# Last layer of a two-layer decoder step: the residual stream and the branch are transposed separately and leave in eight stores

## The reference, cut to what matters

```python
def rms_norm(x, g):
    y = xf * lax.rsqrt(jnp.mean(xf * xf, axis=-1, keepdims=True) + EPS)
    return (y * g).astype(x.dtype)

def cross_sublayer(x, mem_k, mem_v, lp):
    ...
    y = jnp.einsum("bshe,hed->bsd", o, lp["w_xo"])      # 512 -> 2048
    return x + rms_norm(y, lp["norm_x_post"])
```

## Time and profile before

| | us |
|---|---|
| median of the runs | 1278.66 |
| profiled execution, its own time | 1275.5 |
| its span, first to last instruction | 1273.8 |
| PE busy in the span | 1186.9 (93%) |
| DVE busy | 888.9 (70%) |
| ACT busy | 637.2 (50%) |
| POOL busy | 164.7 (13%) |

### The profile page before, as it was taken

The page is one execution under the profiler, slowest core; times in us unless marked ns, Lnnn a source line. Parts: engine busy times, 40 slices in busy tenths (PEclk is TensorE's granted clock), DMA queues, the critical chain, the costliest instruction groups (busy, mean ns, idle before and its releaser), DMA issues. The chain is left out here.

```text
span 1273.8 us, 25083 instructions
## 1 busy us (share of the span) xinstructions
PE 1186.9 (93%) x9846; PEld 1089.3 (86%) x9846; DVE 888.9 (70%) x1527; ACT 637.2 (50%) x1099; POOL 164.7 (13%) x278
## 2 busy tenths in 40 slices
PE   5999999999989899998799999999998999999893
PEld 5999999999767899986689999999976789999782
DVE  4679888888757444765677988888886644457635
ACT  5483444444547344554656544444445644446551
POOL 2200101010352000121011010101034300003100
PEclk8998999999999899999989999999999989999997
DMA  8964646474575466795356674646465646669611
GB/s 223 250 164 119 182 130 186 129 190 116 148 217 169 143 180 177 205 291 188 100 131 184 175 213 132 174 133 176 131 190 159 202 119 170 190 173 298 227 35 68
DMA packets 317544, 216.08 MB, mean 170 GB/s; under 512 B 21476, under 2 KB 300368, under 8 KB 316618
## 3 DMA queue, kind: packets, MB, share of 16 engines
q1 hardware_dynamic: 300624, 166.74, 47.4%
q0 software_dynamic: 16480, 47.73, 12.0%
q10 hardware_dynamic: 330, 0.11, 0.0%
HBM read 209.31 MB, written 7.15 MB: 170 GB/s over the span
## 5 line engine op out<-in xcount | busy, mean ns | idle before, releaser
L1810 DVE TENSOR_TENSOR wlo<-stage,whi 128x2048 fp32r<-128x2048 f32 x140 | 320.4, 2289 | 175.2 <-ACT whi L1227 175.1
L1227 ACT ACTIVATE whi<-stage 128x2048 fp32r<-128x2048 f32 (+2 forms) x159 | 274.6, 1729 | 312.9 <-PE U L651 252.7
L649 PE MATMUL U<-Ahi,whi 128*128 128x264 f32 x1152 | 334.4, 290 | 9.8 <-issue 8.0
L650 PE MATMUL U<-Alo,whi 128*128 128x264 f32 x1152 | 328.5, 285 | 0.0
L651 PE MATMUL U<-Ahi,wlo 128*128 128x264 f32 x1152 | 328.0, 285 | 0.0
L649 PEld LDWEIGHTS U<-Ahi,whi 128*128 128x128 f32 x1152 | 219.3, 190 | 10.9 <-issue 8.2
L650 PEld LDWEIGHTS U<-Alo,whi 128*128 128x128 f32 x1152 | 219.5, 191 | 0.0
L651 PEld LDWEIGHTS U<-Ahi,wlo 128*128 128x128 f32 x1152 | 218.1, 189 | 0.0
L1969 DVE SCALAR_TENSOR_TENSOR acc<-uext,cwall,acc 128x256 f32<-128x256 f32 x464 | 188.5, 476 | 0.1
L649 PE MATMUL U<-Bhi,whi 128*128 128x264 f32 x384 | 108.9, 284 | 0.0
L650 PE MATMUL U<-Blo,whi 128*128 128x264 f32 x384 | 108.8, 283 | 0.0
(11 more groups left out here) (415 smaller groups left out, 2206.0 us busy)
## 6 DMA issues: line engine op xcount, KB each, us to landing
stage<-in_w_in SPq DMA_DIRECT2D x76, 1024.0 KB, 5.9
stage<-in_w_out SPq DMA_DIRECT2D x32, 1024.0 KB, 6.2
stage<-in_w_mk SPq DMA_DIRECT2D x8, 1024.0 KB, 6.4
cp<-in_cache_kv_latent POOLq DMA_DIRECT2D x64, 128.0 KB, 3.0
cp<-in_cache_kv_latent SPq DMA_DIRECT2D x64, 128.0 KB, 2.9
stage<-in_w_mv SPq DMA_DIRECT2D x8, 1024.0 KB, 5.6
Kt<-in_cache_mem_k POOLq DMA_DIRECT2D x16, 512.0 KB, 4.9
stage<-in_w_xq SPq DMA_DIRECT2D x8, 1024.0 KB, 7.3
```

The costliest lines, as they stand in the source:

```text
L649: mm(bk[:, 0:cols], whi[:, s, w], hi[:, k, :], start=(k == 0), stop=False)
L650: mm(bk[:, 0:cols], whi[:, s, w], lo[:, k, :], start=False, stop=False)
L1227: return A_(out, in_, ACT.Copy, scale=scale)
L1810: ins = V.tensor_tensor(wlo[:, s, :], stage[:, s, :], whi[:, s, :].bitcast(F32), ALU.subtract)
```

## The change

In the last layer the transposition no longer waits for the finished sum. The stream `xT` (without this branch) is turned to token rows in eight pieces of 128 tokens x 512 features, one piece behind each of the blocks 1 to 8 of the output projection (`x_turn`), and DVE copies each piece into the row tiles `yR[0]`, `yR[1]`. After the last block the gained branch `yg`, not yet multiplied by the factor, is turned in the same eight pieces (`y_turn`), and DVE forms factor x branch + stream straight from the bank (`y_rows`), with the factor as one number per partition, since a token is now a partition. For that the sums of squares are made per token on partitions (columns 0 and 1 of `ST`) and, for the 8 sample tokens, as before (columns 2 to 9); root and reciprocal are 128 x 10 instead of 128 x 264. The sample tokens keep the old way in one multiply and one add over 16 x 8 elements, 16 transposes and four ACT copies. Every piece has its own store of 256 KB (rows of 2 KB), `ysN` a ninth store. Layer 0 is unchanged.

```diff
-    yN = at("yN", [P, 2, D], A0)
+    yR = [at(f"yR{t}", [P, D], (M, A0 + 4096)[t]) for t in range(2)]
...
+    def turn_bank(i):
+        return (HA, HB, HC, HD, HE)[i % 5]
...
-        sp.wait_ge(fin_act, 8)
-        sp.wait_ge(fin_dve, 8)
-        sp.dma_start(O["yp"].rearrange("a (t p) d -> p (a t) d", p=P), yN[:, :, :]).then_inc(st_y, 16)
+        y_d = O["yp"].rearrange("a (t p) d -> p (a t) d", p=P)
+        for i in range(8):
+            q, t = i // 2, i % 2
+            sp.wait_ge(fin_dve, 9 + i + (2 if i >= 2 else 0))
+            sp.dma_start(y_d[:, t, 512 * q:512 * q + 512], yR[t][:, 512 * q:512 * q + 512]).then_inc(st_y, 16)
+        sp.wait_ge(fin_act, 4)
         sp.dma_start(O["ys"].rearrange("b s d -> (b s) d"), ysN[:, :]).then_inc(st_y, 16)
-        sp.wait_ge(st_y, 32)
+        sp.wait_ge(st_y, 16 * 9)
...
+            def x_turn(i):
+                q, t = i // 2, i % 2
+                if i >= 5:
+                    pe.wait_ge(fin_dve, i - 4)
+                for c in range(4):
+                    last = tr(turn_bank(i)[:, c * P:(c + 1) * P], xT[:, 4 * q + c, t * P:(t + 1) * P], ident[:, :])
+                last.then_inc(fin_mm, 1)
...
                     last.then_inc(unit_done.sem if q == 3 else xo_mm.sem, 1)
-            squares(1)
-        pe.wait_ge(x_upd.sem, x_upd.at(L - 1, 8))
+                    if l == L - 1 and 1 <= bl <= 8:
+                        x_turn(bl - 1)
+            if l < L - 1:
+                squares(1)
+        def y_turn(i):
+            q, t = i // 2, i % 2
+            pe.wait_ge(u_evac.sem, u_evac.at(L - 1, U_XO + 4 * q + 4))
+            if i < 5:
+                pe.wait_ge(fin_dve, (6, 7, 8, 4, 5)[i])
+            elif i == 7:
+                pe.wait_ge(fin_dve, 9)
+            bk = (HA, HB, HC, HD, HE, U[0], U[1], HA)[i]
+            for c in range(4):
+                last = tr(bk[:, c * P:(c + 1) * P], yg[:, 4 * q + c, t * P:(t + 1) * P], ident[:, :])
+            last.then_inc(fin_mm, 1)
+        y_turn(0)
+        y_turn(1)
+        pe.wait_ge(std.sem, std.at(L - 1, 6))
+        pe.wait_ge(ssq_add.sem, ssq_add.at(L - 1, 28))
+        pe.wait_ge(sq_last.sem, sq_last.at(L - 1, 2))
+        for t in range(2):
+            mm(ST[:, t:t + 1], ssq[:, t * P:(t + 1) * P], ones[:, 0:1], start=True, stop=False)
+            mm(ST[:, t:t + 1], sqt[:, 3, t * P:(t + 1) * P], ones[:, 0:1], start=False, stop=True)
+        mm(ST[:, 2:2 + NB], ones[:, :], ssq[:, TP:T], start=True, stop=False)
+        mm(ST[:, 2:2 + NB], ones[:, :], sqt[:, 3, TP:T], start=False, stop=True).then_inc(stat.sem, 1)
+        for i in range(2, 8):
+            y_turn(i)
         pe.wait_ge(std.sem, std.at(L - 1, 7))
-        for c in range(KC):
...
+        pe.wait_ge(fin_dve, 12)
+        for q in range(4):
+            if q:
+                pe.wait_ge(fin_dve, (10, 13, 14)[q - 1])
+            for c in range(4):
+                last = tr((ST, HB, HC, HD)[q][0:NB, c * P:(c + 1) * P], xT[:, 4 * q + c, TP:T], ident[:, :])
+            last.then_inc(fin_mm, 1)
...
+        A_(stdS[:, 0:2 + NB], ST[:, 0:2 + NB], ACT.Sqrt, scale=1.0 / D, bias=epsv[:, 0:1]).then_inc(std.sem, 1)
+        for q in range(4):
+            act.wait_ge(fin_mm, 17 + q)
+            copy(ysN[:, 512 * q:512 * q + 512], (ST, HB, HC, HD)[q][0:NB, :]).then_inc(fin_act, 1)
...
             for bl in range(1, 15):
                 add_squares(1, bl)
+                if l == L - 1 and bl <= 8:
+                    i = bl - 1
+                    q, t = i // 2, i % 2
+                    dve.wait_ge(fin_mm, i + 1)
+                    V.tensor_copy(yR[t][:, 512 * q:512 * q + 512], turn_bank(i)[:, :]).then_inc(fin_dve, 1)
...
+        V.reciprocal(rs[:, 0:2 + NB], stdS[:, 0:2 + NB]).then_inc(rsq.sem, 1)
+        def y_rows(i):
+            q, t = i // 2, i % 2
+            row = yR[t][:, 512 * q:512 * q + 512]
+            dve.wait_ge(fin_mm, 9 + i)
+            V.scalar_tensor_tensor(row, (HA, HB, HC, HD, HE, U[0], U[1], HA)[i][:, :], rs[:, t:t + 1], row, ALU.mult, ALU.add
+                                   ).then_inc(fin_dve, 1)
+        y_rows(0)
+        y_rows(1)
+        dve.wait_ge(u_evac.sem, u_evac.at(L - 1, NG))
+        V.tensor_tensor(yg[:, :, TP:T], yg[:, :, TP:T], bc(rs[:, 2:2 + NB].unsqueeze(1), [P, KC, NB]), ALU.mult
+                        ).then_inc(fin_dve, 1)
+        dve.wait_ge(fin_dve, 11)
+        V.tensor_tensor(xT[:, :, TP:T], xT[:, :, TP:T], yg[:, :, TP:T], ALU.add).then_inc(fin_dve, 1)
+        for i in range(2, 8):
+            y_rows(i)
```

More of the change, by code:

```diff
@@ L1207, in _ @@
                     last.then_inc(unit_done.sem if q == 3 else xo_mm.sem, 1)
-            squares(1)
-        pe.wait_ge(x_upd.sem, x_upd.at(L - 1, 8))
-        pe.wait_ge(std.sem, std.at(L - 1, 7))
-        for c in range(KC):
[L1214 to L1219, removed]
+                    if l == L - 1 and 1 <= bl <= 8:
[25 more added lines that the diff above has]
+            y_turn(i)
+        pe.wait_ge(std.sem, std.at(L - 1, 7))
+        pe.wait_ge(fin_dve, 12)
[5 more added lines that the diff above has]
+            last.then_inc(fin_mm, 1)
     @block.scalar
@@ L1768, in _ @@
                 act.wait_ge(st_mk[e], l * 64 + 64)
[L1769 to L1775, removed]
+            if l < L - 1:
+                root(stat.at(l, 8), l, rsq.at(l, 6), 1.0 / D)
+        act.wait_ge(stat.sem, stat.at(L - 1, 8))
+        act.wait_ge(rsq.sem, rsq.at(L - 1, 6))
+        A_(stdS[:, 0:2 + NB], ST[:, 0:2 + NB], ACT.Sqrt, scale=1.0 / D, bias=epsv[:, 0:1]).then_inc(std.sem, 1)
+        for q in range(4):
+            act.wait_ge(fin_mm, 17 + q)
+            copy(ysN[:, 512 * q:512 * q + 512], (ST, HB, HC, HD)[q][0:NB, :]).then_inc(fin_act, 1)
     @block.vector
@@ L2403, in _ @@
                     lo(0, 0, ll=l + 1)
+            if l == L - 1:
+                break
             dve.wait_ge(u_evac.sem, u_evac.at(l, NG))
@@ L2407, in _ @@
                 residual(1, q)
-                if l + 1 < L and q:
+                if q:
                     next_lower(q - 1)
             assert ch.k == CHAIN_LAYER, ("CHAIN_LAYER", ch.k)
[L2412 to L2416, removed]
+        dve.wait_ge(std.sem, std.at(L - 1, 7))
+        V.reciprocal(rs[:, 0:2 + NB], stdS[:, 0:2 + NB]).then_inc(rsq.sem, 1)
+        dve.wait_ge(rsq.sem, rsq.at(L - 1, 7))
+        def y_rows(i):
[13 more added lines that the diff above has]
+            y_rows(i)
     block.__exit__(None, None, None)
```

## The result

The changed kernel took 1266.31 us in the median of five runs (1262.34 to 1267.96), beside 1278.58 us for five runs of the kernel before: the ratio is 0.9908 (95% interval 0.9889 to 0.9927). On the median that the prediction started from, this is 1266.9 us. Forecast were 1263.5 us and a range up to 1266.8. It is faster, as said, but by 3.4 us less, and the time lies a little outside the range. The profiled execution took 1266.42 us, with a span of 1264.7.

A forecast was written before the change was run, and what follows sets the result against it. Bounds: PE in the projection, then 30.65 us of PE, DVE and DMA in sequence. New end 1255.3 plus 3.3 for turns is 1258.6 against 1273.8; 15.2 off 1278.66 gives 1263.5 us, range 1260.8 to 1266.8.

The forecast's parts named there:

- The chain behind the projection: From the last product through factor, rows on DVE and stores: the span would end about 12.2 us after that product.
- The small products: Six PE products summing squares per token before the root: 0.11 us each, bounds 0.06 and 0.2.
- The rate of the stores: Moving each 256 KB piece out: 0.77 us, fast bound 0.66, slow bound 1.0.
- the gap: Between DVE's second and third pieces, two operations for the sample tokens: together 0.6 us.
- The landing: After the last byte: some 1.2 us until SP sees it landed, then the span's end, 1255.3.
- DVE's pieces: Eight row pieces formed on DVE after the factor: 0.74 us each, 0.66 when nothing is waited for.
- the sample tokens off the path: Their 16 transposes and ACT copies would end at about 1249.8, ahead of piece 7, hidden by DVE's work.
- The projection: Output projection, bound by PE: eight stream turns of 0.44 us, less 0.2 at block 8, lengthen it by 3.3 us.
- block 12's split: DVE's weight split for block 12 in the output projection: not late, by 0.6 us.
- The saving: Whole kernel: span end 1258.6 against 1273.8, 15.2 us less.
- the last step of the sum: Whole kernel: the 15.2 us saving taken off the earlier runs' median, 1278.66, giving 1263.5.
- the first rival: Turns at 0.66 us (+2.0), store pieces at 1.0 (+1.7), or both (+3.7): 1265.2 to 1267.2 us; chance 20%.

The follow-up runs named there:

- again_after: The changed kernel run once more, unaltered: 1262.70 us in the median of six runs, ratio 0.9885 to the kernel before.
- third_after: The changed kernel run again, unaltered, on the chip of later runs: 1264.13 us in the median of five runs, ratio 0.9887 to the kernel before.

## Why the prediction was right, and where it was wrong

**The chain behind the projection: right in sum, by errors that cancel.** The factor came 0.57 us late and the bytes took 0.54 longer, and the end behind the last byte took 0.8 less; of these, 0.3 are left. That the sum is so close is in part luck. All against the end of the last product:

| step | forecast, us | measured, us |
|---|---|---|
| factor ready | 2.25 | 2.82 |
| first store issued | 3.05 | 3.62 |
| first byte | 3.9 | 4.48 |
| last piece formed | 8.15 | 8.72 |
| last byte | 10.55 | 11.67 |
| end of the span | 12.15 | 12.46 |

- The small products were mis-sized. I took a transpose's 0.11 for each; they stand 0.22 us apart, since each is two matmuls (x2 in the rows above): 1.26 us for six, to the end of the last, where 0.83 was taken. That is a little over the upper bound of 0.2 for one. The turns ahead of them began 0.15 later than forecast.
- The rate of the stores was mis-sized a little: 7.19 us and not 6.65, which is 0.84 per piece for 0.77 once the gap and the small store are taken off. By the rate for 256 KiB in the Trainium skill, "SBUF — State Buffer", section "The DMA setup-cost knee", an estimate is 9.4: that rate is for one transfer at a time, and here several are under way, one issued every 0.66 us.
- The landing was mis-sized the other way: 0.8 us from the last byte to the end of the span, where 1.6 had been taken. This was a misreading of the kernel before: by its transfers' own records the burst ended 0.25 us before SP saw it landed, not 1.2, and 0.71 before the end of the span.
- DVE's pieces, their pitch of 0.66 and the sample tokens off the path came as forecast; the gap is 0.5 for 0.6.

**The projection: right.** 3.25 us more, 3.3 forecast; a turn costs 0.43 to 0.44, and nothing waits for block 12's split: DVE ends it at 1245.76, 0.55 before PE comes to the block.

**The saving: right in size, a little too large.** From the first product to the end the kernel before takes 54.39 and 53.25 us in its two profiles, the changed one 39.43, 39.45 and 39.44: 13.8 to 15.0 less, 15.2 forecast. The medians of the 40 runs of the kernel before that stood beside the experiments, 1278.34, and of all 16 of the changed one, 1263.57, differ by 14.8. That is as much as the stretch from the first product gives, so nothing is left for a delay ahead of it that would be the change's own.

**What failed is the last step of the sum**, "I take the saving off the median". It takes for granted that what the change does not touch is the same in each execution, ahead of the projection and in the old tail. The old tail moves by 1.15 us with the clock in its transposes (30.68 and 29.53). The part ahead moves by 7: the projection starts anywhere from 1219.4 to 1226.7 in 14 profiles. Of the 3.4 us between 1266.9 and 1263.5, the saving taken too large is 0.2 to 1.4, and the rest, by subtraction, lies ahead of the projection. A median of three or five such runs moves with it, and the range had room for this on the lower side alone (2.0 off the 1262.2, which is 1260.2 and not the 1260.8 that the prediction wrote), and none on the upper side, where it even stopped at 1266.8, short of the first rival's 1267.2. With the ratios of the two repetitions, 0.9885 and 0.9887, the time would be 1264.0 and 1264.2.

One thing stays open: the four slowest of the 16 runs of the changed kernel all belong to the first five. Its code was the same each time, so it is something of those executions or of their chip; it did not show in the kernel before (1274.22 to 1279.51 there, 1272.61 to 1283.53 over all 40). Two of the four have the lowest mean clocks of all 16 (0.974, 0.975), the other two do not (0.978, 0.980).

## What to carry to other kernels

Read a change's worth between two marks that it cannot touch ahead of, here the first product and the end of the span: that gave 39.43, 39.45 and 39.44 us where whole runs gave 1260 to 1268. Read it in more than one profile, for such a stretch can move too: 54.39 and 53.25 in the kernel before. Give a range the scatter of few runs on both sides. When a result has to leave the chip, turn and store it in pieces as it comes about: the bytes' time behind the first piece then sets the end, so what counts is how early the first piece goes, more than how fast the later ones follow. Work that waits for nothing new (the stream's transposes) belongs into waits that are already there.

## What the runs showed of the hardware that was not expected

- A float32 product of 128 x 1 costs PE 0.22 us at the full clock, twice the pitch of a transpose of 128 x 128 (0.11), and shows as two matmuls.
- Stores from 128 partitions, about 2.16 MB: 6.26 us in two transfers with rows of 8 KB, 6.46 in four with 4 KB, 7.08 to 7.44 in eight with 2 KB. Eight transfers of 32 partitions each with rows of 8 KB took 9.20 us, and SP up to 1.25 us for one issue.
- One packet of such a store took 0.339 us in the mean with 8 KB, 0.164 with 4 KB and 0.101 with 2 KB, so two of 2 KB (0.202) cost more than one of 4 KB, and two of 4 KB about as much as one of 8 KB.
- The time ahead of the projection varied by up to 7 us between executions, and by 5.7 us between two of the same kernel, with the time PE spent at the lower of its two levels (34 to 48 us at 1.2 GHz in place of 2.4) and with PE's idle time (49.9 to 53.7 us).
- In one stretch of the same kernel a wait of PE of 3.40 us was followed by 3.4 us at the lower level, waits of 2.04 and 2.5 us (again_after, third_after) were not. In the two profiles of the kernel before, the granted clock rose from 0.50 to 1.00 in the midst of transposes (at 1262.8 and at 1261.1, PE having done nothing else since 1256.9 and 1257.6).
